# Part of layer 1's input projection ahead of its norm, and residuals, squares and a third weight granule in other places, in a two-block transformer kernel

## What is computed

```python
for i in range(DEPTH):
    hc = modulate(rms_norm(x_ctx, g_norm1[i]), csh1, csc1)
    h  = modulate(rms_norm(x_lat, g_norm1[i]), sh1, sc1)     # h * (1 + scale) + shift
    u = h @ w_in                       # q, k, v, cq, ckv, kr, pool_in
    ...                                # two attentions, and for pool_in:
    op = multiscale_pool(pool_in, w_pool[i], ls_pool[i])     # window means of latent tokens
    x_lat = x_lat + gt1 * (concat(og, om, op) @ w_out[i])
    x_lat = x_lat + gt2 * sq_relu_mlp(modulate(rms_norm(x_lat, g_norm2[i]), sh2, sc2), w_mlp1[i], w_mlp2[i])
    # not in the last layer: the same for x_ctx
```

## Time and profile before

| | |
|---|---|
| median of 3 runs | 1783.94 us (1783.71 to 1788.31) |
| profiled execution | 1790.94 us, span 1789.1 us |
| PE busy | 1733.3 us, 97% of the span |
| DVE, ACT, POOL busy | 63%, 52%, 26% |
| traffic | 255.30 MB, mean 143 GB/s |

### The profile page before, as it was taken

One profiled execution on the slowest core, in us unless ns is written; L12 is line 12 of the kernel. 1 busy time (PEld: TensorE's weight loads), 2 busy tenths in 40 slices (PEclk: granted clock), 3 DMA queues, 4 the chain that ended last, 5 costly groups with the idle time before them and its releaser, 6 DMA issues.

```text
span 1789.1 us, 29093 instructions
## 1 busy us (share of the span) xinstructions
PE 1733.3 (97%) x10840; PEld 1430.9 (80%) x10840; DVE 1135.2 (63%) x2025; ACT 930.6 (52%) x1987; POOL 462.9 (26%) x864
## 2 busy tenths in 40 slices
PE   7999998999999998988999999999999999999998
PEld 3453565888888885647999989899899898998998
DVE  4228874887878433586555578676555777785555
ACT  3237653535353524575555666576554665664542
POOL 0117001000000010330000016257671144387730
PEclk8999999999999998999999999999999999999999
DMA  8323223455555321202455543433345434333351
GB/s 342 140 94 142 95 95 117 166 188 188 188 188 188 137 78 47 95 1 95 142 188 189 186 173 131 163 115 142 142 142 189 158 138 167 140 120 141 123 191 42
DMA packets 106039, 255.30 MB, mean 143 GB/s; under 512 B 2462, under 2 KB 7212, under 8 KB 102828
## 3 DMA queue, kind: packets, MB, share of 16 engines
q1 hardware_dynamic: 104902, 251.16, 38.9%
q0 software_dynamic: 704, 2.10, 0.3%
q10 hardware_dynamic: 294, 0.18, 0.0%
HBM read 252.38 MB, written 1.05 MB: 142 GB/s over the span
## 4 chain that ended last, share of the span: by engine, by line
PE 50%; DVE 1%; ACT 1%; issue 0%; DVEq 0%; ACTq 0%
PE ps L1194 13%; PE ps L1196 12%; PE ps L1195 12%; PE ps L1428 1%; PE ps L1430 1%; PE ps L1429 1%; PE ps L1538 1%; PE ps L1541 1%; PE ps L1533 1%; PE ps L1106 1%; PE ps L1079 1%; PE ps L1504 1%; DVE big_r L2143 0%; PE ps L1517 0%; PE ps L1518 0%; PE ps L1516 0%
## 5 line engine op out<-in xcount | busy, mean ns | idle before, releaser
L2143 DVE TENSOR_TENSOR big_r<-ring,big_r 128x1024 fp32r<-128x1024 f32 x214 | 263.0, 1229 | 253.9 <-ACT big_r L1647 253.6
L1647 ACT ACTIVATE big_r<-ring 128x1024 fp32r<-128x1024 f32 x214 | 226.2, 1058 | 380.3 <-PE ps L1196 360.5
L1195 PE MATMUL ps<-big_r 128*128 128x256 f32 (+1 forms) x1080 | 358.3, 332 | 0.0
L1194 PE MATMUL ps<-hT_r,big_r 128*128 128x256 f32 (+1 forms) x864 | 275.2, 318 | 0.0
L1196 PE MATMUL ps<-hT_r,big_r 128*128 128x256 f32 (+1 forms) x864 | 270.1, 313 | 0.0
L1194 PE MATMUL ps<-big_r 128*128 128x256 f32 (+1 forms) x720 | 240.0, 333 | 2.0 <-DVE big_r L2356 1.4
L1196 PE MATMUL ps<-big_r 128*128 128x256 f32 (+1 forms) x720 | 237.9, 330 | 0.0
L944 POOL TENSOR_TENSOR sq<-sq 128x256 f32<-128x256 f32 (+1 forms) x30 | 37.6, 1252 | 734.9 <-ACT sq L1607 734.7
L1195 PEld LDWEIGHTS ps<-big_r 128*128 128x128 f32 x1080 | 205.3, 190 | 18.6
L1196 PEld LDWEIGHTS ps<-hT_r,big_r 128*128 128x128 f32 x864 | 164.5, 190 | 9.6
L1194 PEld LDWEIGHTS ps<-hT_r,big_r 128*128 128x128 f32 x864 | 164.7, 191 | 9.2
(11 more groups left out here) (353 smaller groups left out, 4240.0 us busy)
## 6 DMA issues: line engine op xcount, KB each, us to landing
ring<-in_w_in SPq DMA_DIRECT2D x44, 2048.0 KB, 7.8
ring<-in_w_mlp SPq DMA_DIRECT2D x32, 2048.0 KB, 7.9
ring<-in_w_mod SPq DMA_DIRECT2D x24, 2048.0 KB, 7.5
ring<-in_w_out SPq DMA_DIRECT2D x4, 2048.0 KB, 8.4
ring<-in_w_out_a SPq DMA_DIRECT2D x4, 2048.0 KB, 7.9
ring<-in_w_out_b SPq DMA_DIRECT2D x4, 2048.0 KB, 8.0
ring<-in_w_o SPq DMA_DIRECT2D x4, 2048.0 KB, 7.7
ring<-in_w_in SPq DMA_DIRECT2D x2, 1152.0 KB, 11.6
```

Of the source, the lines that this page charges most:

```text
L1194: mm(b[:, 0:T], w_hi[:, k, :], hi(k), start=(j == 0), stop=False)
L1195: mm(b[:, 0:T], w_hi[:, k, :], lo(k), start=False, stop=False)
L1647: act_fn(hi, raw, ACT.Copy).then_inc(hi_ready, 1)
L2143: V.tensor_tensor(lo, raw, hi.bitcast(F32), ALU.subtract).then_inc(lo_ready, 1)
```

## The change

Six edits. (1) In the last "down" block of layer 0 ACT also scales chunk k of `xT` (latent tokens) by the norm's gain into `ahead` (`unshifted`). In layer 1 PE multiplies p0 and p1 from `ahead` right behind the squares, before the norm is there. DVE multiplies the result with the root, and POOL adds the product of the shift, which DVE (`shift_products`) and two small matmuls make. (2) In layer 1 the key unit k comes first among the units and q0 after it, with other banks, and the slots of w_in are given back by other products. (3) In the w_out loop DVE does the residual before the low halves, and the first granules of "up" are rounded and split at other steps. (4) In the last "down" block of each layer ACT squares chunk k-1 before it waits for product k and rounds a granule. (5) The third granule of "up" takes part in the product in step, at every second chunk. (6) `hi_to` in the w_out loop is now called at every k.

```diff
@@ units_a, last_product
+    if i:
+        return [("k", "norm", [3]), ("q0", "norm", [2]), ("q1", "norm", [0]), ("q2", "norm", [1]), ("cq", "norm", [3, 2]),
+                ("ckv", "norm", [0]), ("v", "copy", [1]), ("kr", "copy", [3])]
...
-        return [(a, "k", 0), (a, "v", 0), (a, "p1", 0)][n]
+        return [(a, "q2" if i else "k", 0), (a, "v", 0), (a, "kr" if i else "p1", 0)][n]
@@ GpSimd, ahead of the pooling
+                if i:
+                    await_drained(pool, (tag, "shifted"))
+                    for c in range(2):
+                        u = upad[:, c, 1, PAD:PAD + SEQ]
+                        link(nc.gpsimd.tensor_scalar(u, u, small[:, 24 + c:25 + c], None, ALU.add))
@@ TensorE, split_products_in_step
                 for k in range(KC):
                     await_chunk(k)
+                    chunk(0, k)
+                    chunk(1, k)
+                    if third and k == 1:
+                        pe.wait_ge(lo_ready, n0 + 3)
+                    if third and k % 2 and k < KC - 1:
+                        chunk(2, k // 2)
+                for k in range(KC // 2 - 1, KC if third else 0):
+                    chunk(2, k)
@@ TensorE, start of layer 1
                     summed_squares((tag, "n1"), TOK)
+                    w = slot(("win", i, 2))
+                    for c in range(2):
+                        cols = slice(MROPE + P * c, MROPE + P * (c + 1))
+                        b = start_bank((tag, f"p{c}", 0))
+                        for k in range(KC):
+                            pe.wait_ge(ahead_made, k + 1)
+                            last = mm(b[:, 0:SEQ], w[:, k, cols], ahead[:, k, :], start=(k == 0), stop=(k == KC - 1))
+                        fill(last, (tag, f"p{c}", 0))
+                    b = start_bank((tag, "shifted"))
+                    pe.wait_ge(shift_summed, KC)
+                    for c in range(2):
+                        last = mm(b[:, 2 * c:2 * c + 2], shifted[:, c * P:(c + 1) * P], cc("ones", n=2), start=True, stop=True)
+                    fill(last, (tag, "shifted"))
@@ ScalarE, w_out loop (AHEAD_MLP = (3, 4))
                     hi_to(split_by(key))
                     square_summed((tag, "n2"), k, key, t0)
-                    if k in (5, 6):
-                        hi_to(first_gran["mlp", i] + (1 if k == 5 else MLP_BUFS + 1))
+                    hi_to(first_gran["mlp", i] + max(0, AHEAD_MLP[i] + k - KC))
+                g0 = first_gran["mlp", i]
+                hi_to(g0 + 3)
                 reciprocal_root((tag, "n2"), P, TOK - t0, D)
@@ ScalarE, MLP loop
                     key = granules[g][2]
+                    if key[1] == "down" and key[2] == BLOCKS - 1 and key[3] > 0:
+                        square_summed(after, key[3] - 1, (tag, "down", BLOCKS - 1, key[3] - 1), t0)
+                        if i == 0:
+                            unshifted(key[3] - 1)
+                        if i == DEPTH - 1:
+                            gained(0, key[3] - 1)
                     await_bank(act, key)
                     hi_to(split_by(key))
                     if key[1] == "down" and key[2] == BLOCKS - 1 and key[3] > 0:
-                        square_summed(after, key[3] - 1, (tag, "down", BLOCKS - 1, key[3] - 1), t0)
-                        if i == DEPTH - 1:
-                            gained(0, key[3] - 1)
@@ VectorE, w_out loop
                 for m in range(KC):
+                    residual((tag, "wout", m), m, i, 16, s0)
                     lo_to(split_by((tag, "wout", m)))
-                    residual((tag, "wout", m), m, i, 16, s0)
...
-                    if m >= 5:
-                        lo_to(g0 + m - 4)
+                    if i and m == KC - 2:
+                        lo_to(g0 + 1)
+                lo_to(g0 + 3)
@@ VectorE, MLP loop
                         residual(key, key[3], i, 40, s0)
+                        if i == 0 and key[2] == BLOCKS - 1 and key[3] >= KC - 2:
+                            shift_products(*((0, 4) if key[3] == KC - 2 else (4, KC)))
```

More of the change, by code:

```diff
@@ L605, in program @@
         roped = sem("roped")
+        ahead_made = sem("ahead_made")
+        shift_summed = sem("shift_summed")
         pooled = sem("pooled")
@@ L1197, in split_product, with split_products_in_step, chunk @@
                 fill(last, key)
-            def split_products_in_step(n0, hi, lo, T):
-                keys = [granules[n0 + g][2] for g in range(2)]
+            def split_products_in_step(n0, hi, lo, T, third=False):
+                keys = [granules[n0 + g][2] for g in range(2 + third)]
                 banks = [start_bank(key) for key in keys]
+                def chunk(g, k):
+                    w_hi, w_lo = gran_bufs[n0 + g]
+                    b = banks[g][:, 0:T]
+                    mm(b, w_hi[:, k, :], hi(k), start=(k == 0), stop=False)
+                    mm(b, w_hi[:, k, :], lo(k), start=False, stop=False)
+                    last = mm(b, w_lo[:, k, :], hi(k), start=False, stop=(k == KC - 1))
+                    if k == KC - 1:
+                        fill(last, keys[g])
                 pe.wait_ge(lo_ready, n0 + 2)
@@ L1205, in split_products_in_step @@
                     await_chunk(k)
-                    for g in range(2):
-                        w_hi, w_lo = gran_bufs[n0 + g]
-                        b = banks[g][:, 0:T]
-                        mm(b, w_hi[:, k, :], hi(k), start=(k == 0), stop=False)
-                        mm(b, w_hi[:, k, :], lo(k), start=False, stop=False)
-                        last = mm(b, w_lo[:, k, :], hi(k), start=False, stop=(k == KC - 1))
-                        if k == KC - 1:
-                            fill(last, keys[g])
+                    chunk(0, k)
[6 more added lines that the diff above has]
+                    chunk(2, k)
             def plain_product(key, w, m, cols, src, T):
@@ L1685, in late_reduced, with unshifted @@
                 drain(last, key)
+            def unshifted(k):
+                if k == 0:
+                    act.wait_ge(modA_made, 2)
+                act_fn(ahead[:, k, :], xT[:, k, LAT:TOK], ACT.Copy, scale=amod[:, 1, 0, k, 1:2]).then_inc(ahead_made, 1)
             def mod_row_copied(n):
@@ L2186, in modulated_norm, with shift_products @@
                         h_rest(i, k, s0)
+                return n
             nt_free = []
             n_rot = [0]
+            def shift_products(k0, k1):
+                n = slot_no["win", 1, 2]
+                dve.wait_ge(slot_landed[n % RING], landed_at[n])
+                for k in range(k0, k1):
+                    w, c = ring[:, n % RING, k, MROPE:MROPE + 2 * P], mod[:, 1, k, 1:2]
+                    if k == 0:
+                        V.tensor_scalar(shifted, w, c, None, ALU.mult).then_inc(shift_summed, 1)
+                    else:
+                        dve.wait_ge(shift_summed, k)
+                        V.scalar_tensor_tensor(shifted, w, c, shifted, ALU.mult, ALU.add).then_inc(shift_summed, 1)
             def apply_norm(tag, name):
@@ L2271, in _ @@
                     mod_scaled(0, 8, RA["g1"], 0, modA_made)
-                modulated_norm(i, 0, 0, i == 0)
+                root = modulated_norm(i, 0, 0, i == 0)
+                if i:
+                    dve.wait_ge(padded, i + 1)
+                    for c in range(2):
+                        key = (tag, f"p{c}", 0)
+                        await_bank(dve, key)
+                        drain(V.tensor_tensor(upad[:, c, 1, PAD:PAD + SEQ], bank(key)[:, 0:SEQ], rstd[:, root % 2, LAT:TOK],
+                                              ALU.mult), key)
                 if i == 0:
```

22 lines of the change are left out of this document (19 added, 3 removed).

## The result

The changed kernel takes **1773.68 us** (median of 5 runs, 1768.66 to 1775.43) against 1788.10 us for the kernel before in the same rounds (1783.71 to 1790.2). The ratio is 0.9916, 95% interval 0.9898 to 0.9934, so the change saves 12 to 18 us. Repeated in another set it was 0.9912 (0.9895 to 0.9929), with medians of 1770.89 and 1785.07 us. The forecast was a saving of 15.7 us, the absolute number 1768.2 us in a range of 1763.5 to 1773.0. The saving by medians is 14.4 us (14.2 in the other set), close to the forecast, and the time lies 0.7 us above the range. Of the 5.5 us between 1768.2 and 1773.68, 4.2 are the level: the forecast was hung on 1783.94, the median of three runs of the kernel before, and with two more runs that median is 1788.10. The other 1.3 are saving that did not come.

The account below looks back on a forecast made before the run. PE was taken as the bound, so only its idle time counted. 5.6 + 10.6 + 2.0 - 2.5 = 15.7 us, taken from 1783.94, gave 1768.2 us, range 1763.5 to 1773.

Parts of the forecast that it names:

- Second norm, layer 0: Layer 0's second norm: root and first chunk 5.5 us sooner, plus 0.1 us for the third granule; 5.6 us saved.
- the bunched squares: Layer 0's second norm: roundings bunched at k = 0 delay squares, but POOL's sums end about when product 7 does; no cost.
- the third granule: "Up" granule in step at the second norms: layer 0 saves 0.1 us, 2.0 as other bound; layer 1 loses 0.3.
- First norm, layer 1: Layer 1's first norm: PE multiplies pooled columns while it would wait, then k ahead of q0; 10.6 us saved.
- k, p0 and p1 done, q0 lacking: Layer 1's first norm, at 689 us: 14.1 us of products done, q0's 3.5 us lacking; 10.6 us gained.
- slot late: Rival, layer 1's first norm: DVE waits for the third slot ahead of chunk 7's residual; 1773.4 us, chance 0.08.
- pooled columns' place needed: Rival, layer 1 from kr to qm0: ACT and DVE set the pace, 7.07 us given back; 1775.3 us, chance 0.06.
- clock low in p0 and p1: Rival, layer 1's first norm: clock falls during these products; 1770.1 us, chance 0.15 together with full speed at layer 0's second norm.
- Second norm, layer 1: Layer 1's second norm: POOL's sum done at 840.7, root 2.3 us sooner, third granule costs 0.3; 2.0 us saved, bounds 0 and 3.
- Last down block: Layer 1's last "down" block: ring of rounding, residual, square and gained chunk takes 3.5 us against 2.88; 2.5 us lost.

Follow-up runs that it names:

- e1_both: Changed kernel with no MLP rounding ahead of its turn and, in layer 1's last down block, square and gained copy behind the rounding again; 1766.2 us, ratio 0.9889.
- e3_queries_first: Changed kernel with q0 ahead of k in layer 1, pooled columns still first, banks not exchanged; 1779.72 us, ratio 0.9975.
- e1_squares_back: Changed kernel with square and gained copy behind the rounding again in the last down block of layer 1 only; 1767.87 us, ratio 0.9898.
- e1_paced: Changed kernel, but ACT rounds nothing for the MLP ahead of its turn in the w_out loops; 1767.6 us, ratio 0.9897.

## Why the prediction was right in the saving and off in the time

- **Second norm, layer 0 (5.6).** Right: 6.2. Root and first chunk came 5.8 us sooner (forecast 5.5), the bunched squares cost nothing there, and the third granule gave 0.4, near the 0.1 taken and far from the 2.0 of the full clock. The granted clock was 0.60 and 0.50 from the first chunk to 300.2.
- **First norm, layer 1 (10.6).** Right, 10.9, and by the route that was given: k was done 17.2 us behind product 7 (forecast 17.45). The count of "k, p0 and p1 done, q0 lacking" rests on PE being busy up to the first chunk, and so at full clock: keys first was worth nothing behind an idle wait and 1.8 behind the pooled columns. The earlier squares, which the forecast did not price by themselves, are 2.9 of the sum. The risks priced there (slot late, pooled columns' place needed, clock low in p0 and p1) did not come. The slot was close, by 0.2 us.
- **Second norm, layer 1 (2.0).** This is the step that failed: 2.0 forecast, 0.5 lost in the pair of traces, nothing won in any. The text saw the bunch of squares but took POOL's sum to end 1.8 us behind the last product and the root to start 2.8 behind it. They came 2.6 and 3.9 behind it, so the root was 1.2 us sooner instead of 2.3. The third granule cost 0.65, not 0.3. That leaves some 0.5 won. It was lost because the lower clock behind the first chunk lasted 5.6 us against 3.9, and 1.7 us more at half the clock are some 0.85 us of work (an estimate from the two traces). The forecast took an earlier root for a gain in full and had no term for that stretch, but its length differs as much between executions of one code, so that this change made it longer is not shown. What removes the late sum, pacing the roundings, gives 1.9 us.
- **Last down block (-2.5).** Right: 2.5 lost between R and D, 3.45 us per granule as against the 3.5 forecast, and 2.8 won back by the edit that undoes it. PE's waits show as 0.28 to 0.35 us, not 0.6. The starts of its matmuls tell the rest: they stand 0.12 us apart and 0.63 at such a wait (1002.88 to 1003.51), so 0.5 us are lost each time.
- **The sum.** 15.7 forecast, 14.6 in the trace, 14.2 to 15.7 by the times. The step above is off by 2.5, and 0.6 each at layer 0 and in the rest and 0.3 at the first norm hide more than half of that, which no term had foreseen: in part luck. The level is the other miss: 1783.94 from three runs, against 1788.10 from five runs that include them, and 1784.46 to 1785.23 in the later sets. Either miss alone would have left the time inside the range, and in the second set the changed kernel's 1770.89 is inside it. The range had no room for both, though the text itself had repeats 4.6 us apart. A range for an absolute time has to hold the level's own spread.

## What to carry to other kernels

Cut both traces at places that every version has, and compare the stretches between them, since kernels with the same code up to a place differed there by 8 us. Then look at the same stretch in every trace that has its code: one pair showed 3.0 us where the edit was worth 1.9. A call that means "nothing yet" in a running count may still do all the work that is outstanding: read what the engine then waits for. A product that fills a wait of PE is worth its own time plus what the lower clock would have cost behind the wait, and a product moved into the slow stretch behind a wait is worth less than its time.

## What the runs showed of the hardware beyond that

The level of an execution goes with stretches where the granted clock is sometimes lower, sometimes not, in the same code. The windows of `e1_both`, and those of `e3_queries_first`, whose program is the same up to there:

```profile
20.00:40.00 20.00, 17.88 (x87) 0.75 0.89 356
40.00:60.00 20.00, 20.00 (x45) 0.82 0.78 269
```

```profile
20.00:40.00 20.00, 17.84 (x100) 1.00 1.01 385
40.00:60.00 20.00, 20.00 (x47) 1.00 0.70 243
```

A is at 292.1 in the first and at 284.9 in the second. Over the traces it lies between 284.9 and 292.8 us (the two runs with work added at the start left out), early where that clock is 1.00. The transfers go the same way (a DMA share of 0.89 against 1.01 from 20 to 40 us), so whether the clock or the transfers come first is open. The same happens in layer 1's attention: the window of 740 to 760 us shows 1.00 in the changed kernel and 0.91 in `e1_squares_back`, and Q to C is 100.1 and 102.4 us:

```profile
740.00:760.00 20.00, 15.17 (x75) 1.00 0.00 0
```

```profile
740.00:760.00 20.00, 15.53 (x56) 0.91 0.00 1
```

Together that is about the spread of one kernel's runs (1765.0 to 1772.0 us for `e1_squares_back`). That it is the cause of the spread is argued from single traces, not shown. The Trainium skill (the same page and part) says that how many products run at the lower clock varies from run to run of one kernel; the traces agree, with the windows above.

POOL's sum of 256 columns took 0.73 us in some rows and 1.47 in others of one kernel, and 1.1 on average in the bunch of six. In `e1_paced` the sum at 811.87 has no DVE operation beside it and takes 0.73. Those at 809.45 and 818.09 start 0.36 us into one of DVE's low halves (1.23 us, from two tiles in SBUF) and take 1.47.
